# A two-layer streaming encoder step on one core: some weight transfers cut by partitions into two

## The reference, cut to what matters

```
def trunk_layer(x, ple, pos, lp, lb, cache):
    proj = x @ lp['w_in']
    ...                                   # attention a, recurrence o
    merged = jax.nn.sigmoid(ga) * (a @ lp['w_br_a']) + jax.nn.sigmoid(gb) * (o @ lp['w_br_b'])
    x = layernorm(DN_ALPHA * x + merged @ lp['w_out'], lp['ln1_g'], lp['ln1_b'])
    moe_out = hier_moe(x, lp['w_rg'], lp['w_re'], lp['w1'], lp['w3'], lp['w2'])
    ple_term = jax.nn.sigmoid(x @ lp['w_ple_gate']) * (ple @ lp['w_ple'])
    x = layernorm(DN_ALPHA * x + moe_out + ple_term, lp['ln2_g'], lp['ln2_b'])

def expert_block(args):
    xb, e = args
    h = jax.nn.silu(xb @ w1[e]) * (xb @ w3[e])      # w1, w3: 1024 x 512
    return h @ w2[e]                                # w2: 512 x 1024
```

## Time and profile before

| what | value |
|---|---|
| median of three runs | 1562.12 us |
| the profiled execution's own time | 1561.42 us |
| its span, first to last instruction | 1559.6 us |
| bytes moved, mean rate over the span | 490.85 MB, 315 GB/s |
| rate in the expert stage | 427 GB/s |
| time in queue q1 (SP's transfers), share of 16 engines | 74.8% |
| PE busy | 83% of the span |
[...]

### The profile page before, as it was taken

How to read it: one execution, slowest core, us unless ns; L and a number is a source line. 1 busy time by engine, 2 the same in 40 slices (tenths; PEclk the granted TensorE clock), 3 DMA queues, 4 the chain that set the end, 5 groups by cost and what they waited for, 6 DMA issues and landing times.

```text
span 1559.6 us, 20228 instructions
## 1 busy us (share of the span) xinstructions
PE 1295.5 (83%) x8504; PEld 724.0 (46%) x8505; DVE 402.4 (26%) x1031; ACT 264.8 (17%) x692; POOL 57.0 (4%) x100
## 2 busy tenths in 40 slices
PE   7999999999976766766799999999998766667654
PEld 4766887554431321321276668776353322213311
DVE  4141642541111101101133437245222011011003
ACT  3342422020100000000044324211110000000001
POOL 1300000000000000000022010000000000000000
PEclk9999999999988978988899999999999879879887
DMA  9403425889999999999972034469999999999994
GB/s 327 159 1 108 170 95 196 367 339 427 425 426 427 427 426 427 426 427 426 407 219 82 1 120 158 168 216 392 370 427 426 426 427 426 427 427 425 427 426 166
DMA packets 100047, 490.85 MB, mean 315 GB/s; under 512 B 9553, under 2 KB 15601, under 8 KB 52465
## 3 DMA queue, kind: packets, MB, share of 16 engines
q1 hardware_dynamic: 94912, 476.46, 74.8%
q0 software_dynamic: 5040, 13.03, 2.7%
HBM read 486.56 MB, written 2.89 MB: 314 GB/s over the span
## 4 chain that ended last, share of the span: by engine, by line
PE 55%; DMA 35%; SPq 7%; DVE 2%; issue 1%; ACT 0%; POOL 0%; DVEq 0%
PE bank L973 53%; DMA arena<-in_w_e_gate 12%; DMA arena<-in_w_e_up 7%; DMA ring<-in_w_e_up 7%; SPq L769 4%; DMA ring<-in_w_e_down 4%; DMA arena<-in_w_e_down 4%; SPq L835 2%; PE bank L1023 2%; DMA ring<-in_w_in 1%; DVE arena L1917 0%; DVE x_sb L1926 0%; DVE arena L2029 0%; ACT xT L1555 0%; DVE arena L2061 0%
## 5 line engine op out<-in xcount | busy, mean ns | idle before, releaser
L973 PE MATMUL bank<-arena 128*32 128x512 f32 (+10 forms) x2744 | 503.2, 531 | 126.8 <-DMA arena<-in_w_e_gate 33.0
L973 PEld LDWEIGHTS bank<-arena 128*32 128x32 f32 (+5 forms) x2744 | 194.5, 140 | 339.6 <-issue 326.7
L973 PE MATMUL bank<-ring,arena 128*32 128x512 f32 (+4 forms) x1376 | 343.0, 645 | 2.7 <-ACT arena L1866 2.7
L973 PE MATMUL bank<-ring,xT 128*32 128x128 f32 (+5 forms) x1536 | 240.7, 375 | 1.3 <-ACT xT L1555 1.1
L973 PE MATMUL bank<-xT,ring 128*128 128x288 f32 x768 | 191.8, 407 | 0.0
L973 PEld LDWEIGHTS bank<-ring,xT 128*32 128x32 f32 (+1 forms) x1536 | 124.3, 142 | 101.5 <-issue 90.0
L973 PEld LDWEIGHTS bank<-xT,ring 128*128 128x128 f32 x768 | 143.7, 190 | 37.9
L973 PE MATMUL bank<-cst,arena 128*32 128x512 f32 x144 | 88.1, 770 | 59.2 <-DMA arena<-in_w_e_up 25.6
L973 PEld LDWEIGHTS bank<-ring,arena 128*32 128x32 f32 (+1 forms) x1376 | 86.7, 129 | 43.3 <-issue 34.1
L973 PE MATMUL bank<-arena,x_sb 128*128 128x128 f32 (+1 forms) x768 | 99.7, 282 | 1.4 <-DVE arena L2248 0.8
L973 PEld LDWEIGHTS bank<-arena,x_sb 128*128 128x128 f32 (+1 forms) x768 | 90.5, 190 | 19.8 <-issue 13.1
(11 more groups left out here) (224 smaller groups left out, 846.8 us busy)
## 6 DMA issues: line engine op xcount, KB each, us to landing
arena<-in_w_e_gate SPq DMA_DIRECT2D x68, 1024.0 KB, 25.9
arena<-in_w_e_up SPq DMA_DIRECT2D x62, 1024.0 KB, 26.3
arena<-in_w_e_down SPq DMA_DIRECT2D x58, 1024.0 KB, 26.5
ring<-in_w_e_up SPq DMA_DIRECT2D x48, 1024.0 KB, 26.6
ring<-in_w_e_gate SPq DMA_DIRECT2D x44, 1024.0 KB, 26.5
ring<-in_w_e_down SPq DMA_DIRECT2D x42, 1024.0 KB, 26.7
ring<-in_w_in SPq DMA_DIRECT2D x32, 1024.0 KB, 9.7
lb<-in_w_e_gate SPq DMA_DIRECT2D x14, 1024.0 KB, 25.8
```

Source lines behind the costliest of these rows:

```text
L973: return pe.matmul(out, lhsT, rhs, start=first, stop=last, skip_group_check=True)
```

## The change

Some pieces are no longer one transfer but two, which differ in the partitions they fill. A table SPLIT_ROWS gives, for a piece number, how many partitions the first of the two has. For the last four pieces it is 120, in each of the eight blocks: a transfer of 120 partitions and one of 8. For k = 96, 97 and 98 it is 104, 88 and 72, so the second transfers have 24, 40 and 56 partitions. The bytes are the same. Both transfers add 16 to the same semaphore, so FILLS counts two for such a piece, and PE waits for twice the number on `last_full`.

```diff
+SPLIT_ROWS = {QUADS * len(MOE_PIECES) - QUAD + e: 120 for e in range(QUAD)}
+SPLIT_ROWS.update({4 * len(MOE_PIECES) + e: rows for e, rows in enumerate((104, 88, 72))})
...
-            count[i] += 2 if last[i] is not None and first_released(last[i]) else 1
+            k = len(slots) - 1 - layer * LAYER_PIECES - len(PIECES)
+            count[i] += 2 if k in SPLIT_ROWS or last[i] is not None and first_released(last[i]) else 1
...
+                    n = layer * LAYER_PIECES + len(PIECES) + k
+                    if k in SPLIT_ROWS:
+                        await_slot(n)
+                        in_parts(slot(n), experts[w][g * QUAD + e, :, h, :], SPLIT_ROWS[k], ring_full[SLOT_OF[n]])
+                        return
...
+                def in_parts(dst, src, rows, signal):
+
+                    sp.dma_start(dst[0:rows, :], src[0:rows, :]).then_inc(signal, 16)
+                    sp.dma_start(dst[rows:P, :], src[rows:P, :]).then_inc(signal, 16)
...
-                            sp.dma_start(slot(n)[:, D * c:D * c + D], src).then_inc(last_full if c else ring_full[SLOT_OF[n]], 16)
+                            in_parts(slot(n)[:, D * c:D * c + D], src, SPLIT_ROWS[k], last_full if c else ring_full[SLOT_OF[n]])
...
-                                pe.wait_ge(last_full, 16 * QUAD * (layer + 1))
+                                pe.wait_ge(last_full, 2 * 16 * QUAD * (layer + 1))
```

More of the change, by code:

```diff
@@ L807, in load_expert @@
                     w, h, e = MOE_PIECES[i]
+                    n = layer * LAYER_PIECES + len(PIECES) + k
[3 more added lines that the diff above has]
+                        return
                     src = experts[w][g * QUAD + e:g * QUAD + e + 1, :, h, :].rearrange("e p n -> p e n")
-                    load(layer * LAYER_PIECES + len(PIECES) + k, 1, SLOT, src)
+                    load(n, 1, SLOT, src)
+                def in_parts(dst, src, rows, signal):
+                    sp.dma_start(dst[0:rows, :], src[0:rows, :]).then_inc(signal, 16)
+                    sp.dma_start(dst[rows:P, :], src[rows:P, :]).then_inc(signal, 16)
                 def load_blocks(ks):
```

## The result

The changed kernel takes 1614.29 us (median of four runs, 1608.58 to 1618.89) against 1561.38 us for the kernel before (1560.53 to 1562.82): +52.9 us, ratio 1.0336, 95% interval 1.0302 to 1.037. I had forecast +4.4 us, with 1570.0 as the upper end of the range. The direction was right, the size wrong by a factor of twelve.

The account below looks back on a forecast made before the run. The prediction took DMA transfers in both expert stages as the bound, ending when the last engine finishes. +2.2 us per layer, two layers +4.4, gave 1565.8 us on the profiled basis, 1566.5 for the median; range 1559.3 to 1570.0.

Parts of the forecast that it names:

- DMA bounds both expert stages, and the last landing is handed on: Both expert stages: transfers set the pace at 427 GB/s; each layer's last landing shift passes nearly one for one, twice.
- Shares: equal, of whole partitions, on as many engines as divide them: Split transfers: 120 goes as 8 partitions to 15 engines, 104 as 13 x 8, 8 as one to each of 8.
- the rival of level shares: Split transfers: shares level to one partition over all sixteen engines; 1560.7 us or 1566.4; chance 0.22.
- A packet takes 0.307 us, or 0.153, whatever transfer it belongs to: All weight transfers: at 26.7 GB/s per engine, an 8 KB packet takes 0.307 us and a 4 KB one 0.153.
- 8 x 0.307: Mid-stage pieces: first ten engines have 32 packets instead of 24, 2.5 us more per layer.
- The term of the end: Eight last blocks: first eight engines get one 4 KB packet more per block, 8 x 0.153 us per layer.
- What an engine is behind by in mid-stage it keeps: Mid-stage to layer end: an engine's delay persists, since all sixteen are busy until the end.
- Between best case 1.4 and worst 3.7, reliefs wasted: Layer ends: loaded engines delay the end 1.4 to 3.7 us, taken as +2.2; most relief of five engines wasted.
- plateau at 10 or 11: Second layer's tail, a sign: a DMA share near 10 or 11 of 16 engines should last longer.
- The other parts cost nothing on the path: SP's extra issues, slot waits and PE's doubled count: covered by queued transfers, cover about 10 us at layer end.
- if mid-stage waits of PE or DVE grow by more than 2.5 us in all, I have missed a path: Mid-stage, a sign: growth of PE or DVE waits above 2.5 us in all would mean an overlooked path.
- Issue limit: Layer ends: sixteen SP issues at 2.15 us last 34.4 us, landings +1.9 and +3.2 us, 1567.2 us; chance 0.08.

Follow-up runs that it names:

- experiment 1: Changed kernel with only the three mid-stage pieces of a layer split (104/24, 88/40, 72/56), last blocks whole: 1589.52 us, ratio 1.0168.
- 11: Kernel before, with only the eight last blocks of a layer split, by columns over all 128 partitions: 1562.66 us, ratio 1.0001.
- 12: Kernel before with only mid-stage pieces split, into three forties and an eight: forties of neighbouring partitions 1594.29 us; of every third partition 1589.3 us.
- 13: Kernel before with only mid-stage pieces split, into four parts of 32 neighbouring partitions: ascending order 1578.37 us; order 0, 64, 32, 96 1576.2 us.
- experiment 2: Changed kernel with only the eight last blocks of a layer split (120 and 8), mid-stage pieces whole: 1580.77 us, ratio 1.0123.
- experiment 3: Changed kernel's eleven split transfers per layer cut by columns instead, each part on all 128 partitions: 1560.77 us, ratio 1.0002.
- Experiment 4: Changed kernel with SPLIT_ROWS 64 for all eleven transfers of a layer, partitions 0 to 63 and 64 to 127: 1596.62 us, ratio 1.0216.
- 8: Splits at 64 partitions, first part reading even source rows, second odd: 1594.34 us; or first part filling even partitions, second odd: 1561.75 us.
- 9: Kernel before, no splits, mid-stage pieces and last blocks reading 128 neighbouring source rows instead of every second: 1560.67 us, ratio 0.9994.
- experiment 10: Two mid-stage pieces per layer as sixteen transfers of 16 neighbouring partitions: sorted (groups 0, 2 of both, then 1, 3...) 1583.87 us; mixed, piece by piece, 1571.07 us.
- 5: Changed kernel with parts in multiples of 16 partitions: SPLIT_ROWS 112 for the blocks and 112, 96, 80 for the pieces: 1600.03 us, ratio 1.0241.
- 6: One mid-stage piece per layer as eight transfers of 16 rows: into neighbouring partitions 1566.61 us, ratio 1.0035; into every eighth partition 1569.54 us, ratio 1.0049.

## Why the prediction was wrong

A rule made after experiments 1 to 11, and on record before 12 and 13: count the packets of the busiest engine in the split part, take twice the old time for each, and subtract the old total. In us, for both layers (experiments 1 to 11 are fitted by it, only 12 and 13 test it):

| split | rule | lost |
|---|---|---|
| as changed | 2 x (32 x 0.614 - 7.4 + 72 x 0.307 - 9.8) = 49.1 | 52.9 |
| mid-stage only / end only | 24.6 / 24.6 | 28.1 / 19.4 |
| halves / 112, 96, 80 | 34.4 / 34.4 | 35.2 / 38.6 |
| one piece 104 and 24 | 2 x (10 x 0.614 - 2.46) = 7.4 | 9.7 |
| forties in order / quarters in order | 33 / 14.7 | 33.2 / 17.3 |
| columns; even and odd partitions | 0 | 0 |
| sixteen rows of one piece: neighbours / every eighth | 4.9 / 0 | 5.2 / 8.1 |
| two pieces in sixteens: sorted / mixed | 9.8 / 9.8 | 22.5 / 9.7 |
| forties spread / quarters alternating | 9.2 / 14.7 | 28.3 / 15.2 |

The rule holds within some 5 us for parts of neighbouring partitions in their usual order. It fails three times: for every eighth partition and for the forties spread, where spread parts are counted at the old packet time, and for the sorted order. The factor of two is rounded as well: the halves' rate gives 427/246 = 1.7.

That the direction came out right was mostly luck: halves with equal shares, for which the prediction's account gives +0, lose 35.2 us. By the steps of the prediction:

- *DMA bounds both expert stages, and the last landing is handed on.* Right. PE starts the next layer at 808.31, 4.95 us after its last block of the first ends (796.87 + 6.49), as before (776.35 to 781.30); so the next layer's loads were in time, as predicted.
- *Shares: equal, of whole partitions, on as many engines as divide them.* The packet counts bear out the number of engines to the unit (160 more), and exclude the rival of level shares, which would give 224.
- *A packet takes 0.307 us, or 0.153, whatever transfer it belongs to.* This is the step that failed. They took about 0.65 in mid-stage. With the same count of packets for the busiest engine, 32 in mid-stage instead of 24, the term "8 x 0.307", 2.5 us, becomes by the rule 32 x 0.614 - 24 x 0.307 = 12.3 us. The rates give 12.3 and 14.1 us in the changed kernel, 11.6 and 13.7 in experiment 1. The term of the end, put at 8 x 0.153 = 1.2, becomes 12.3 by the rule; it was 13.7 and 16.3 in the changed kernel, and 19.4 for both layers together in experiment 2. I named ends for what no row showed of the shares, but took the packet's time from whole transfers without any bound, though no row had a partial one.
- *What an engine is behind by in mid-stage it keeps.* The tail of experiment 1, twice as long with whole last blocks, speaks for it in the second layer (3.9 us); in the first its landing is no later than mid-stage's loss, so this is not shown throughout.
- *Between best case 1.4 and worst 3.7, reliefs wasted.* Both ends rest on the same packet time. That relief of five engines buys nothing is right in its outcome. Engines leave early, as forecast, but there is no plateau at 10 or 11: 12 to 13 for 4 us, 9.6 for 2, then one or two for some 5 us.
- *The other parts cost nothing on the path.* For SP's issues and the doubled counts this is right (experiment 3). But the sentence "if mid-stage waits of PE or DVE grow by more than 2.5 us in all, I have missed a path" came true. PE's waits for expert weights are 85.6 us between 450 and 735 us before and 97.9 in the same work after (450 to 747.3 us); in the second layer 85.0 (1200 to 1500) and 97.3 (1227 to 1541). That is +24.6 us in mid-stage; over the whole run, ends included, they go from 187.1 to 234.2. What was missed is no new path but the packet time on the known one. The row that grew most, in the first and in the second layer, first before, then after (total, times, longest):

```profile
PE bank L973 <- DMA arena<-in_w_e_gate: 17.8, 5, 6.2
PE bank L973 <- DMA arena<-in_w_e_gate: 16.5, 5, 6.1
```
```profile
PE bank L988 <- DMA arena<-in_w_e_gate: 28.1, 5, 9.3
PE bank L988 <- DMA arena<-in_w_e_gate: 24.4, 4, 13.1
```

- *Issue limit.* Excluded by experiment 3 and by issues of 0.31 us. The sixteen took 26.4 and 30.1 us where I had said 22 to 28; I take the rest to be waiting for room in a slow queue.
- *Only unequal shares cost.* The prediction has no term for a split that leaves the shares equal. Experiment 4 puts halves at +35.2 us for 14 MB: they ran at 246 to 248 of 427 GB/s.

**The mechanism.** Shown: the loss comes with the cut by partitions and not with the number of transfers (experiment 3). For the halves it is made at the destination (8, 9), by packets that take 1.7 times as long at a share of 1.0. It depends on which partitions make up a part (8), and for parts of sixteen on their order in the queue (10).

Not isolated is how much of the changed kernel's own loss belongs to what. Parts of neighbouring partitions with equal shares lose 35.2 and 38.6 us (4, 5). The other 14 to 18 of the 52.9 go with the unequal shares; the rule gives 49.1 - 34.4 = 14.7 for them, but no run has them alone. The one run that changes the destination of unequal parts (12) lost 28.3 us instead of 33.2, with overlapping intervals.

Why one set of partitions is slow and another is not, no run shows. The runs fit neither a count of the partitions in a part nor how far apart they lie. Of parts of 64, the neighbouring ones ran at 246 GB/s and the even ones at 424; 120 of 128 partitions, nearly all of them, at 242 (experiment 2). Spread parts lost in 12 (229 GB/s) and in 6 (+8.1 us, against +5.2 for neighbours) and not in 8. The order made a difference for sixteens (22.5 against 9.7 us) and none for quarters (17.3 against 15.2). How a partial transfer's rows are dealt to the engines, and how many packets an engine keeps under way, stays open too; that engines get in each other's way at the destination is a reading, not a result.

Also open: the price of unequal shares alone. No run has extra rows on chosen engines and nothing else. And why mid-stage costs 2 us more in the second layer than in the first (13.7 against 11.6 in experiment 1, 14.1 against 12.3 in the changed kernel), and why only the second layer's tail grew in experiment 1.

## What to carry to other kernels

Where transfers bound a kernel, keep every large one on all 128 partitions and split it by columns if it must be split: columns cost nothing here (experiment 3, ratio 1.0002), while partitions 0 to 63 and 64 to 127 apart ran at 246 of 427 GB/s. When a change gives transfers a shape that no row of the trace has, the time of one packet is an unknown too and needs a bound from above; count the busiest engine's packets, and price them both at their old time and at twice it (the worst order here, in experiment 10, had 427/170 = 2.5 times). A DMA share of 1.0 does not say how much the engines move: here it stood beside 427 GB/s (1.01) and beside 170 (1.03, experiment 10). Read it with the GB/s.

## What the runs showed of the hardware

- Splits of neighbouring partitions: 180 (changed kernel) to 250 GB/s (quarters) in most stretches of 10 us at a DMA share of about 1.0, against 427 for whole ones; 170 when sixteen-partition parts stand in the sorted order of experiment 10. Other pieces in flight are slowed as well: from 530 to 552 us of the changed kernel 4.52 MB took 0.65 us per packet, of which at most 3.1 MB are split pieces.
- The same transfers split by columns: 1560.77 us, ratio 1.0002, no loss.
- Even and odd partitions apart: 424 GB/s, 1561.75 us, no loss. Every third partition, on ten engines (229 GB/s, +28.3 us), and every eighth (+8.1 us) do lose. The order of the source rows made no difference: whole transfers from rows 8 KB apart 1560.67 us (ratio 0.9994), halves from every second row 1594.34 us, as the halves' 1596.62.
- One short packet more per engine used and transfer: +160, +352 (halves), +132 (forties) in the page's packet count. With the engine counts of the prediction it comes out to the unit.
- An issue of SP takes as little as 0.31 us (0.38 at the start, with next to nothing queued); with many transfers queued 2.1 us and more (2.10 for one and 10.51 for three).
